# Expert weights of a mixture-of-experts stage: one load per expert into a ring of three places, addressed by a register

## What is computed

```python
def _moe(h, w_gr, b_gr, w_er, b_er, w_eg, w_eu, w_ed):
    t = h.reshape(-1, D_MODEL)                      # D_MODEL = 1024
    pg = jax.nn.softmax(t @ w_gr + b_gr, axis=-1)
    gi = jnp.argmax(pg, axis=-1)                    # top-1 group
    ...
    tw, ti = lax.top_k(jax.nn.softmax(el, axis=-1), TOP_K)   # top-2 experts of the group
    ...
    hg = jnp.einsum('nd,edf->nef', t, w_eg)         # 16 experts, 1024 x 256
    hu = jnp.einsum('nd,edf->nef', t, w_eu)
    a = jax.nn.silu(hg) * hu * comb[..., None]
    out = jnp.einsum('nef,efd->nd', a, w_ed)        # 256 x 1024
```

## Time and profile before

| | us |
|---|---|
| median of 3 runs | 2105.66 |
| lowest and highest | 2099.86 and 2107.53 |
| span of the profiled execution | 2103.6 |
| PE busy with matmuls, in the span | 1718.4 (82%) |
| gate-up matmuls (line 2097), 512 instructions | 256.2 |
| down matmuls (line 2116), 256 instructions | 116.4 |
| DMA, hardware queue q1: 336.85 MB | 47.7% of 16 engines' span |

### The profile page before, as it was taken

One profiled execution on the slowest core, in us unless ns is written; L12 is line 12 of the kernel. 1 busy time (PEld: TensorE's weight loads), 2 busy tenths in 40 slices (PEclk: granted clock), 3 DMA queues, 4 the chain that ended last, 5 costly groups with the idle time before them and its releaser, 6 DMA issues. The chain is left out here.

```text
span 2103.6 us, 30608 instructions
## 1 busy us (share of the span) xinstructions
PE 1718.4 (82%) x11079; PEld 1064.3 (51%) x11079; DVE 732.0 (35%) x1167; ACT 431.1 (20%) x755; POOL 285.6 (14%) x392
## 2 busy tenths in 40 slices
PE   5999998789886988888599999799448898789920
PEld 3444446444444656555399999644224343344410
DVE  2110119344553433343354554254421111111138
ACT  1000011244432222222043343101101111011113
POOL 0000010100002111110032231022300000000034
PEclk8999999777777999999699999999769989899965
DMA  8323420000005999999354545521059878879944
GB/s 309 116 101 103 162 85 3 1 1 0 0 0 172 385 387 387 387 387 387 109 141 120 143 115 134 191 87 70 26 199 313 280 255 283 290 258 325 306 156 155
DMA packets 276134, 385.44 MB, mean 183 GB/s; under 512 B 18220, under 2 KB 175549, under 8 KB 276054
## 3 DMA queue, kind: packets, MB, share of 16 engines
q1 hardware_dynamic: 262904, 336.85, 47.7%
q0 software_dynamic: 8560, 30.97, 4.3%
q10 hardware_dynamic: 4608, 16.78, 2.0%
HBM read 354.48 MB, written 30.07 MB: 183 GB/s over the span
## 5 line engine op out<-in xcount | busy, mean ns | idle before, releaser
L2097 PE MATMUL ps<-we_w_gu,ex_xT 128*128 128x512 f32 x512 | 256.2, 659 | 57.0 <-DMA we_w_gu<-w_exp_up 55.4
L326 PE MATMUL ps<-w_w,g_arena 128*128 128x512 f32 x512 | 228.4, 605 | 7.6 <-issue 4.0
L2097 PEld LDWEIGHTS ps<-we_w_gu,ex_xT 128*128 128x128 f32 x512 | 106.8, 212 | 202.9 <-issue 200.6
L1503 PE MATMUL ps<-mix_x_hi,mix_w_hi 128*128 128x352 f32 x576 | 188.7, 328 | 18.5 <-DVE mix_x_lo L1467 16.8
L1503 PE MATMUL ps<-mix_x_hi,mix_w_lo 128*128 128x352 f32 x576 | 186.9, 324 | 0.0
L1503 PE MATMUL ps<-mix_x_lo,mix_w_hi 128*128 128x352 f32 x576 | 186.5, 324 | 0.0
L1133 PE MATMUL ps<-g_ident,sat_k_pg 128*128 128x128 f32 x1024 | 129.0, 280 | 42.7 <-DMA sat_k_pg<-cache_k 38.7
L326 PEld LDWEIGHTS ps<-w_w,g_arena 128*128 128x128 f32 x512 | 97.6, 193 | 127.2 <-issue 125.9
L1133 PEld LDWEIGHTS ps<-g_ident,sat_k_pg 128*128 128x128 f32 x1024 | 113.9, 144 | 75.6 <-issue 70.1
L1545 DVE TENSOR_TENSOR mix_w_lo<-mix_w_raw,mix_w_hi 128x1024 fp32r<-128x1024 f32 x73 | 125.9, 1756 | 32.9 <-ACT mix_w_hi L1530 25.0
L1102 ACT COPY sat_kT<-ps 128x512 f32<-128x512 f32 x128 | 73.5, 587 | 249.7 <-PE ps L1133 249.7
(11 more groups left out here) (371 smaller groups left out, 2140.7 us busy)
## 6 DMA issues: line engine op xcount, KB each, us to landing
sat_k_pg<-cache_k SPq DMA_DIRECT2D x256, 256.0 KB, 7.9
sat_v_pg<-cache_v SPq DMA_DIRECT2D x256, 256.0 KB, 7.9
we_w_gu<-w_exp_gate SPq DMA_DIRECT2D x32, 1024.0 KB
we_w_gu<-w_exp_up SPq DMA_DIRECT2D x32, 1024.0 KB
we_w_dn<-w_exp_down SPq DMA_DIRECT2D x32, 1024.0 KB, 8.3
mix_w_raw<-w_in SPq DMA_DIRECT2D x49, 512.0 KB
g_arena<-w_ada SPq DMA_DIRECT2D x16, 1024.0 KB
y_rows<-ex_y ACTq DMA_DIRECT2D x32, 512.0 KB, 6.8
```

The lines of the kernel that those rows point to most:

```text
L326: last = nc.tensor.matmul(ps[:, b, :], g.hT[:, k, t * P:(t + 1) * P], w[s][:, k, :], start=(k == 0), stop=(k == KD - 1))
L1503: last = nc.tensor.matmul(out, w[p][:, at], v[:, x, :], start=(i == 0 and k == 0), stop=(i == len(w_chunks) - 1 and k == 2))
L2097: last = nc.tensor.matmul(ps[:, 2 + s, :], xT[s][:, k, :], w_gu[s][:, k, :], start=(k == 0), stop=(k == KD - 1))
```

## The change

Each expert's three weights are loaded once, expert 0 first and expert 15 last, into a ring of `RING` = 3 places; expert e uses place e mod 3. The first three are loaded at the start of `route`, without a wait. In `experts` SP goes through the experts: it waits until an expert's three loads have landed and adds one to a new semaphore `w_ready` (`announce`); it waits until all tiles of expert e are through their down matmuls, from a table `expert_ends` made in `route`, and loads expert e+3 into the place that is free.

PE reads two numbers for each tile from a table `tile_plan`: how many announcements its expert needs, and in which place its weights lie. Ahead of gate-up it waits for `w_ready` to reach the first. The second is part of the address of each gate-up and down matmul's moving operand. The waits on `gu_in` and `dn_in` are gone.

For the ring's count of finished tiles to hold, every expert gets at least one tile: the first entry of `steps` becomes -1, so that an expert without tokens counts as one tile. `route` computes the two tables in a chain of small DVE operations in place of `tile_expert`.

```diff
@@ -1822,7 +1822,7 @@
 
-def route(nc, io, g, ps, load_weights):
+def route(nc, io, g, ps, weights):
 
...
@@ -1850,7 +1850,8 @@
         tile_no, past, owner = sb("tile_no", [1, SLOT_TILES]), sb("past", [1, SLOT_TILES, NEXP]), sb("owner", [1, SLOT_TILES])
-        consts, own = m.sem("consts"), m.sem("own")
+        consts, own, steps_set = m.sem("consts"), m.sem("own"), m.sem("steps_set")
+        third, ends_i = sb("third", [1, SLOT_TILES], I32), sb("ends_i", [1, NEXP], I32)
         shifted, exped, counted, sums_read = m.sem("shifted"), m.sem("exped"), m.sem("counted"), m.sem("sums_read")
...
@@ -1858,9 +1859,8 @@
             def _(sp):
-                sp.wait_ge(have_experts, 1)
-                for tile in range(2):
-                    load_weights(sp, tile, tile)
+                for e in range(RING):
+                    weights.load(sp, e)
 
...
@@ -1873,7 +1873,10 @@
                 nc.gpsimd.iota(steps[:], pattern=[[P, NT]], base=0, channel_multiplier=0,
-                               allow_small_or_imprecise_dtypes=True).then_inc(consts, 1)
+                               allow_small_or_imprecise_dtypes=True).then_inc(steps_set, 1)
+                pool.wait_ge(steps_set, 1)
+
+                nc.gpsimd.memset(steps[:, 0:1], -1.0).then_inc(consts, 1)
                 nc.gpsimd.iota(tile_no[:], pattern=[[1, SLOT_TILES]], base=0, channel_multiplier=0,
...
@@ -1968,7 +1971,21 @@
                 link(v.tensor_scalar(owner[:], owner[:], float(NEXP - 1), None, ALU.min))
-                v.tensor_copy(g.tile_expert[:], owner[:]).then_inc(have_experts, 1)
+                link(v.tensor_copy(third[:], owner[:]))
+
+                link(v.tensor_scalar(g.tile_plan[:, :, 1], third[:], 1, None, ALU.add))
+                link(v.tensor_scalar(owner[:], owner[:], 11.0, None, ALU.mult))
+                link(v.tensor_copy(g.tile_plan[:, :, 0], owner[:]))
+                link(v.tensor_scalar(g.tile_plan[:, :, 0], g.tile_plan[:, :, 0], 5, None, ALU.logical_shift_right))
+                link(v.scalar_tensor_tensor(out=g.tile_plan[:, :, 0], in0=g.tile_plan[:, :, 0], scalar=-float(RING),
+                                            in1=third[:], op0=ALU.mult, op1=ALU.add))
+                link(v.tensor_copy(ends_i[:], ends[0:1, :]))
+
+                for s in range(2):
+                    link(v.tensor_scalar(g.expert_ends[:, :, s], ends_i[:], 2 * START + 1 - s, None, ALU.add))
+                v.tensor_scalar(g.expert_ends[:], g.expert_ends[:], 1, None, ALU.logical_shift_right)\
+                    .then_inc(have_experts, 1)
+                dve.wait_ge(have_experts, 1)
 
...
@@ -1992,30 +2009,27 @@
 
+RING = 3
+
+
 class ExpertWeights:
...
         self.nc, self.g = nc, g
-        self.gate_up = [m.sb(f"w_gu{s}", [P, KD, 2 * DE]) for s in range(2)]
-        self.down = [m.sb(f"w_dn{s}", [P, DE // P, D]) for s in range(2)]
-        self.gate_up_in, self.down_in = m.sems("gu_in", 2), m.sems("dn_in", 2)
+        self.gate_up = m.sb("w_gu", [P, RING, KD, 2 * DE])
+        self.down = m.sb("w_dn", [P, RING, DE // P, D])
+        self.arrived = m.sems("w_in", RING)
         self.gate_v = io["w_exp_gate"][0].rearrange("e (k p) f -> e p k f", p=P)
...
 
-    def load(self, sp, tile, s, gate_up_used=None, down_used=None):
-
-        e = sp.value_load(self.g.tile_expert[0:1, bass.ds(tile, 1)], min_val=0, max_val=NEXP - 1)
-        if gate_up_used:
-            sp.wait_ge(*gate_up_used)
+    def load(self, sp, e):
+
+        s = e % RING
         for at, src in ((0, self.gate_v), (DE, self.up_v)):
-            sp.dma_start(self.gate_up[s][:, :, at:at + DE], src[bass.ds(e, 1)].rearrange("a p k f -> (a p) k f"))\
-                .then_inc(self.gate_up_in[s], 16)
-        if down_used:
-            sp.wait_ge(*down_used)
-        sp.dma_start(self.down[s][:], self.down_v[bass.ds(e, 1)].rearrange("a p k f -> (a p) k f"))\
-            .then_inc(self.down_in[s], 16)
+            sp.dma_start(self.gate_up[:, s, :, at:at + DE], src[e]).then_inc(self.arrived[s], 16)
+        sp.dma_start(self.down[:, s], self.down_v[e]).then_inc(self.arrived[s], 16)
 
...
@@ -2032,7 +2046,8 @@
 
-        w_gu, w_dn, gu_in, dn_in = weights.gate_up, weights.down, weights.gate_up_in, weights.down_in
+        w_gu, w_dn, arrived = weights.gate_up, weights.down, weights.arrived
+        w_ready = m.sem("w_ready")
         x, y, who = two("x", [P, D]), two("y", [P, D]), two("who", [P, 1], I32)
...
@@ -2056,11 +2071,21 @@
             def _(sp):
-
-                with sp.Fori(1, LAST + 1) as use:
+                def announce(e):
+                    sp.wait_ge(arrived[e % RING], 48 * (e // RING) + 48)
+                    sp.sem_inc(w_ready, 1)
+
+                announce(0)
+                for e in range(NEXP - RING):
+                    announce(e + 1)
+
+                    done = [sp.value_load(g.expert_ends[0:1, e, s:s + 1], min_val=START, max_val=START + SLOT_TILES)
+                            for s in range(2)]
                     for s in range(2):
-
-                        weights.load(sp, 2 * use + s, s, (gu_full[s], START + use), (y_full[s], START + use))
+                        sp.wait_ge(y_full[s], done[s])
+                    weights.load(sp, e + RING)
+                for e in range(NEXP - RING + 1, NEXP):
+                    announce(e)
 
...
@@ -2087,15 +2112,22 @@
 
+                def slot_of(use, s):
+                    return pe.value_load(g.tile_plan[0:1, bass.ds(2 * use + s, 1), 0], min_val=0, max_val=RING - 1)
+
                 def gate_up(use, s):
+
+                    need = pe.value_load(g.tile_plan[0:1, bass.ds(2 * use + s, 1), 1], min_val=1, max_val=NEXP)
+                    slot = slot_of(use, s)
                     for half in range(2):
                         pe.wait_ge(xT_copied[half][s], START + use + 1)
-                    pe.wait_ge(gu_in[s], 32 * use + 32)
+                    pe.wait_ge(w_ready, need)
 
...
                     for k in range(KD):
-                        last = nc.tensor.matmul(ps[:, 2 + s, :], xT[s][:, k, :], w_gu[s][:, k, :], start=(k == 0),
-                                                stop=(k == KD - 1))
+                        last = nc.tensor.matmul(ps[:, 2 + s, :], xT[s][:, k, :],
+                                                w_gu[:, bass.ds(slot, 1), k, :].rearrange("p a n -> p (a n)"),
+                                                start=(k == 0), stop=(k == KD - 1))
                     last.then_inc(gu_full[s], 1)
...
@@ -2107,14 +2139,15 @@
                 def down(use, s):
+                    slot = slot_of(use, s)
                     pe.wait_ge(aT_copied[s], START + use + 1)
-                    pe.wait_ge(dn_in[s], 16 * use + 16)
                     for half in range(2):
...
                             last = nc.tensor.matmul(ps[:, 6 + half, :], aT[s][:, k, :],
-                                                    w_dn[s][:, k, half * 512:(half + 1) * 512], start=(k == 0),
+                                                    w_dn[:, bass.ds(slot, 1), k, half * 512:(half + 1) * 512]
+                                                    .rearrange("p a n -> p (a n)"), start=(k == 0),
                                                     stop=(k == KE - 1))
...
@@ -2370,7 +2403,7 @@
         g.slot, g.slot_list = m.sb("slot", [P, 2, NT], I32), m.sb("slot_list", [P, SLOT_TILES], I32)
-        g.tile_expert = m.sb("tile_expert", [1, SLOT_TILES], I32)
+        g.tile_plan, g.expert_ends = m.sb("tile_plan", [1, SLOT_TILES, 2], I32), m.sb("expert_ends", [1, NEXP, 2], I32)
         g2 = m.sb("g2", [P, 2, D])
...
@@ -2385,7 +2418,7 @@
             weights = ExpertWeights(nc, io, g, Mem(nc, w_ctx, "we"))
-            route(nc, io, g, ps, weights.load)
+            route(nc, io, g, ps, weights)
             experts(nc, io, g, ps, weights)
```

## The result

| | before | after |
|---|---|---|
| median, us | 2103.13 (2099.86 to 2107.53) | 2069.28 (2063.33 to 2072.93) |
| profiled span, us | 2103.6 | 2071.2 |
| first to last gate-up, us | 438.94 | 402.87 |
| waits of gate-up on weights or their announcement | 55.4 us, 15 | 33.6 us, 6 |

The ratio after to before is 0.983, interval 0.980 to 0.986. The forecast was 2067; it came true, also in its mechanism, though several of its sizes were off and nearly cancelled.

The account below looks back on a forecast made before the run. PE's waits for expert weights (55.4 us in 15) were taken to bound the experts' stage. 82 + 1 - 2 - 42 = 39 us off 2105.7 gave 2067, 2053 to 2082 for this case; overall range 2034 to 2096.

Parts of the forecast that it names:

- to win between the gate-ups: Experts' stage, first to last gate-up: 438.9 us against 31 unwaited steps, 358.4; 80.5 us saved if no waits.
- routing: Routing stage: earlier weight loads and gather against 2.1 us more DVE chain; 1 us gained, ends 2 gained and 1 lost.
- the down's register operation: Down's first matmul, behind the wait for aT: 0 to 0.1 us in 32 tiles; 2 us cost, ends 0 and 3.
- six announcement waits: Gate-ups at tiles 6, 11, 12, 17, 20, 21 wait on SP: six times 7.0, 42 us, ends 31 and 54.
- What bounds, and where the waits go: Experts' stage: PE waits for weights, 55.4 us in 15 waits; afterwards six waits, ended by SP's semaphore.
- The unwaited step: Experts' stage: a tile that doesn't wait takes 11.56 us, with gate-up 7.03 us of it.
- The announcement's wait: PE idles while SP issues three DMAs, 4.0 us: 4.5 us idle, ends 3.4 and 6.1, plus 2.5 slow clock.
- Register loads: PE's value_loads ahead of gate-up and down: hidden under matmuls in the array, costed at nothing.
- The third: Rival, PE: a value_load waits until the array has drained; 2152 us, 2106 to 2190; chance 0.11.
- the second rival: PE's register loads outlast their 3.4 us cover by 0.5 to 1.2 us a tile; 2083 to 2106; chance 0.12.
- The first rival: SP's announcement is cheap, PE idles 1.9 us at each of six; 2043, with no wait 2025; chance 0.16.
- The fourth rival: Experts' stage: weights still come late, some 4 us over at two places; 2075; chance 0.03.

Follow-up runs that it names:

- The first experiment: Changed kernel with SP announcing expert e+2 before it waits for the end of expert e; 2031.45 us, ratio to before 0.963.
- the two experiments on loads: Changed kernel with one, then four, more value_loads and always-met waits ahead of each gate-up; 2071.70 us and 2119.53 us.
- the second experiment: Changed kernel with the announcement moved ahead of the third DMA (down) of the next load; 2032.16 us, ratio to before 0.964.
- the second pair: Kernel before and changed kernel, unaltered, each profiled a second time on one chip; spans 2110.1 and 2067.7 us.
- four more loads: Changed kernel with four more value_loads and met waits ahead of each gate-up; 2119.53 us, ratio to before 1.005.
- two places: Kernel announcing e+2 before expert e's end, with RING = 2 instead of 3 and tile plan's factor 16; 2166.77 us, ratio to before 1.028.
- the bytes twice: Kernel announcing e+2 before expert e's end, each in-stage load repeated into an unread fourth place; 2055.27 us, ratio to before 0.977.

## Why the prediction was right, point by point

| term, us | forecast | measured |
|---|---|---|
| to win between the gate-ups | 80.5 | 85.8 (438.9 - 31 x 11.39) |
| the last gate-up (measured: from its start to the span's end) | 1.8 | 1.6 |
| routing | 1 | 2.1 |
| the down's register operation | -2 | 0 |
| six announcement waits | -42 | -49.8 (402.9 - 31 x 11.39) |
| sum | 39 | 39.7 |

- **What bounds, and where the waits go.** Right. The experts' tiles, the six places, the releaser and the clock behind each wait all came as written. The first experiment shows the cause of four, the second the place in SP's queue, and the times of landing show the hold at all six; the cause had been only argued from the order of the code and two issue rows.
- **The unwaited step was read wrongly.** 11.56 came from the tile at 1595.67, which stood behind a wait of 2.21 us; its gate-up was 7.13, not 7.03. The tile at 1665.27 had the right number in the same rows: the next gate-up starts at 1681.90 behind 5.08 of idle, so the step is 11.55 less the 0.16 by which a down's modelled end overlaps the next gate-up, 11.39. Times 31 that is 5.3 us more to win.
- **The announcement's wait was too short.** I took 4.0 us for the three issues, nearer to the empty queue's 2.88 than to 5.57. The first stall had 4.89 (0.37, 0.58 and 3.85 with gaps), all six 4.6 to 5.7. Idle time was 5.1 to 6.1, forecast 4.5 with ends of 3.4 and 6.1; slow clock 15.3 / 6 = 2.55, forecast 2.5. The whole, 49.8, lies inside the ends 31 and 54. The reason that I gave for the lower value, that nothing else of SP's is in flight, was true and didn't help: the third of three issues on an empty queue was held 3.85.
- **Register loads.** Right that they cost nothing: PE's two loads ran from 1605.91 to 1607.52, with the waits to 1607.73, and the first matmul of the next gate-up came at 1609.05. The third and the second rival fall with that; by the two experiments on loads the second becomes true from 0.5 to 1 us of more register work in a tile. The rows agree with the Trainium skill (Advanced Engine Details and Errata, Sequencer Loop) that control work runs while instructions stand queued. TENSOR_LOAD took 0.29 us on PE (288 ns, 128 of them above; with its register work a load took 0.63), not the 0.6 us that the Trainium skill (DMA: Bandwidth & Descriptors, Latency and other measured facts) gives as a floor; the measurement decides. The down's register operation was hidden too: steps without a wait are as long as before.
- **Routing.** DVE's chain to slot_list grew by 1.95 us (9.66 to 11.61 from the clamp of owner), as forecast. Behind it 4.2 us were won (15.39 to 11.17 from slot_list's end to the first gate-up), not 3.3: from the issue of the first gather to the transposes of its rows it took 4.2 us (1556.74 to 1560.92) and not 5.6 (1550.17 to 1555.79), 1.4 less, where I had given 0.5. The rest is SP's sixth issue, which no longer held up the end of the stage, nearly as forecast.
- **The first rival**, a cheap announcement, was false for this order of the queue, but its price, 2043, was near what the second experiment built (2032).
- **The fourth rival**, late weights, was right to be small here: at tiles 12 and 21 the hold of SP came on top of one step's lead and gave the load time to land. With the hold gone it is true there: 4.98 and 4.52 us.

Errors of some 8 us on either side nearly cancelled: the forecast was right in what happens and lucky in the last half per cent. The medians differ by 33.9 us and the spans by 32.4, in the second pair by 42.4; the earlier stages of one execution move by some 6 us, so the table, which is taken inside the stages, is the better measure of the steps.

## What to carry to other kernels

Where one queue both hands out work and says that work is ready, say first and hand out second: six announcements, each behind three DMA issues, cost 50 us here, and the one line ahead of the third issue would have doubled the gain of the change. A wait for a semaphore names its sender, not its cause; ask what the sender was doing at that moment, and whether the thing announced had long been there. To price an unwaited step, take one that stands behind an unwaited one, and when one wait has been removed look for the next one in its shadow (here two loads that land late), since it shows only then.

## What was not expected of the hardware

- A gap of 1.4 to 2.3 us on PE may or may not be followed by the slow clock. Of the six of 1.4 to 2.2 us in the second experiment none was (gate-up 7.13). Of the 24 bare gaps behind four more loads two of 1.9 us were (8.83 us at 1599.51), others of the same length not. With two places 2.19 and 2.23 were not, and 2.26 was; with the bytes twice 2.10 was (8.83 us at 1685.50). All waits of gate-up of 3.7 us or more were followed by gate-ups longer by 1.5 us at least.
- The third of three 1 MB issues held SP for 3.85 us where nothing else of SP's was in flight, and for 1.4 us at 1647.44 in the first experiment, where SP's load before it had landed too (1645.14). What sets its length stays open.
- Where nine issues follow one another, in the routing of the changed kernel, the sixth ended at 1533.52, and the first three DMAs had landed at 1533.56; in the ten other executions of kernels with the ring the two times lie within 0.06 us of each other as well. This fits the prediction's reading that a long issue is held until the queue has moved some of what it has.
